# Down projection of a decoder layer's feed-forward part: where VectorE takes the bank sums, who makes the weight sums, and when the weight blocks are requested

## What is computed

```python
    mix = jnp.concatenate([y_a, y_b, y_c], axis=-1) @ p['w_out'][l]
    x = x + rmsnorm(mix, p['g_post_mix'][l])
    h = rmsnorm(x, p['g_pre_ffn'][l])
    f = (jax.nn.silu(h @ p['w_gate'][l]) * (h @ p['w_up'][l])) @ p['w_down'][l]
    x = x + rmsnorm(f, p['g_post_ffn'][l])
```

## Time and profile before

| | |
|---|---|
| profiled execution, device time | 1510.76 us |
| its span in the profile | 1509.1 us |
| down projection, steps 0 to 65 | 1227.7 to about 1451 us |
| fourth product in passes, and the end | 1451.8 to 1509.1 us |
| PE busy, whole span | 94% |
| DVE, ACT, POOL busy, whole span | 61%, 35%, 38% |
| mean granted TensorE clock | 0.969 |

### The profile page before, as it was taken

The page is one execution under the profiler, slowest core; times in us unless marked ns, Lnnn a source line. Parts: engine busy times, 40 slices in busy tenths (PEclk is TensorE's granted clock), DMA queues, the critical chain, the costliest instruction groups (busy, mean ns, idle before and its releaser), DMA issues.

```text
span 1509.1 us, 32359 instructions
## 1 busy us (share of the span) xinstructions
PE 1412.9 (94%) x13256; PEld 1317.4 (87%) x13256; DVE 926.6 (61%) x1441; ACT 521.3 (35%) x914; POOL 579.1 (38%) x493
## 2 busy tenths in 40 slices
PE   7999999997999999889969999999999998888995
PEld 6899999996999665548869999999999998887995
DVE  6439888722888446556686455555555564569866
ACT  5422231222332435444452323333332333333452
POOL 4044000004985222200065555555555530249634
PEclk9999999998999999989989999999999999999997
DMA  7222111222543434452202333333333335554533
GB/s 221 64 46 57 31 43 44 65 61 64 155 115 114 137 85 136 124 170 84 88 24 78 98 93 106 106 96 88 106 106 106 106 114 175 154 154 147 157 85 127
DMA packets 145115, 155.76 MB, mean 103 GB/s; under 512 B 18893, under 2 KB 113352, under 8 KB 144953
## 3 DMA queue, kind: packets, MB, share of 16 engines
q1 hardware_dynamic: 117762, 140.44, 30.7%
q10 hardware_dynamic: 24006, 12.12, 3.0%
q0 software_dynamic: 3200, 1.14, 0.6%
HBM read 120.62 MB, written 33.35 MB: 102 GB/s over the span
## 4 chain that ended last, share of the span: by engine, by line
PE 45%; DVE 5%; POOL 2%; issue 2%; ACT 1%; DMA 1%; SPq 0%; DVEq 0%; POOLq 0%; ACTq 0%
PE mf_ps L3167 28%; PE mf_ps L3194 9%; PE mf_ps L3102 6%; PE mf_ps L3207 1%; POOL ff_a L2635 1%; DMA ff_m_raw<-hidden_operands 1%; PE mf_ps L3225 1%; DVE ff_s_lo L2943 0%; DVE h_lo L2891 0%; POOL ff_a L2639 0%; DVE ff_m_lo L2941 0%; DVE ff_p_lo L2937 0%; DVE ff_scaled L2982 0%; PE mf_ps L3112 0%; DVE h_t_lo L2891 0%
## 5 line engine op out<-in xcount | busy, mean ns | idle before, releaser
L3167 PE MATMUL mf_ps<-h_t_hi,ff_w_hi 128*128 128x258 f32 x704 | 144.5, 287 | 8.8 <-DVE h_t_lo L2891 6.3
L3167 PE MATMUL mf_ps<-h_t_hi,ff_w_lo 128*128 128x258 f32 x704 | 142.9, 285 | 0.0
L3167 PE MATMUL mf_ps<-h_lo,ff_w_hi 128*128 128x258 f32 x704 | 142.4, 284 | 0.0
L2886 DVE TENSOR_TENSOR ff_w_lo<-ff_sum,ff_w_hi 128x512 fp32r<-128x512 f32 x88 | 87.2, 991 | 85.9 <-ACT ff_w_hi L2720 83.9
L3194 PE MATMUL mf_ps<-ff_m_hi,ff_s_hi 128*128 128x258 f32 x528 | 111.0, 293 | 22.0 <-DVE ff_acc L2951 10.7
L3167 PEld LDWEIGHTS mf_ps<-h_t_hi,ff_w_hi 128*128 128x128 f32 x704 | 110.9, 192 | 9.4 <-issue 6.5
L813 PE MATMUL pc_main<-h_hi,in_whi 128*128 128x344 f32 x528 | 116.7, 330 | 1.7 <-PEq L88 1.7
L2941 DVE TENSOR_TENSOR ff_m_lo<-ff_m_raw,ff_m_hi 128x516 fp32r<-128x516 f32 x66 | 75.2, 1140 | 65.3 <-ACT ff_m_hi L2753 64.8
L813 PE MATMUL pc_main<-h_lo,in_whi 128*128 128x344 f32 x528 | 113.2, 323 | 0.0
L813 PE MATMUL pc_main<-h_hi,in_wlo 128*128 128x344 f32 x528 | 112.7, 322 | 0.0
L3167 PEld LDWEIGHTS mf_ps<-h_t_hi,ff_w_lo 128*128 128x128 f32 x704 | 110.4, 191 | 0.0
(11 more groups left out here) (494 smaller groups left out, 3626.0 us busy)
## 6 DMA issues: line engine op xcount, KB each, us to landing
ff_m_raw<-hidden_operands SPq DMA_DIRECT2D x66, 258.0 KB, 3.1
fs_keys<-in_cache_k_dram SPq DMA_DIRECT2D x64, 192.0 KB, 2.9
at_values<-in_cache_v_dram SPq DMA_DIRECT2D x64, 192.0 KB, 2.5
hidden_operands<-ff_t_sum SPq DMA_DIRECT2D x44, 258.0 KB, 3.4
ff_raw<-in_w_gate_dram SPq DMA_DIRECT2D x22, 512.0 KB, 5.9
ff_raw<-in_w_up_dram SPq DMA_DIRECT2D x22, 512.0 KB, 5.2
ff_a<-in_w_down_dram SPq DMA_DIRECT2D x44, 256.0 KB, 3.0
in_raw<-in_w_in_dram ACTq DMA_DIRECT2D x20, 512.0 KB, 3.9
```

The costliest lines, as they stand in the source:

```text
L2886: dve.tensor_tensor(w_lo[q % 4][:], stationary(*tasks[q]), w_hi[q % 4][:].bitcast(F32), ALU.subtract).then_inc(w_lo_cut, 1)
L3167: last = pe.matmul(into[:, g], a[q % 4][:, k], b[:, k, g * TQ:(g + 1) * TQ], start=(fresh and k == 0 and i == 0), stop=(k == KH - 1 and i ...
```

## The change

Six things are changed, all in the down projection:

1. At the end of the products FIRST, SECOND, SEVENTH, SIXTH and THIRD, VectorE's `product_out` stands one low-part step earlier: ahead of the low parts of step j + 2, where it stood behind those of step j + 3 (j the product's last step). ScalarE's `fifth_out` moves in the same way. The addition in SBUF that follows the fifth product stays.
2. The 44 stationary sums go from GpSimd to VectorE, one in each iteration (`sum_blocks(j + 4)`), at its head.
3. Weight blocks have semaphores of their own (`block_in`) and are requested three steps ahead, behind the moving operand of the step and not ahead of it.
4. ScalarE casts the stationary block before the moving operand, and VectorE makes their low parts in that order. ScalarE waits itself for the end of step j - 4.
5. The transposes of chunks (`turned_after`) come one or two pass steps earlier.
6. The statistics (`stats_after`) come one to three pass steps earlier.

```diff
         cut_through = lambda j: min(STEPS, j + 4 + max(0, min(3, j - WIDE + 1)))
-        arrived = lambda j: 32 * (j // 4 + 1) if j < 4 * pairs else 32 * pairs + 16 * (j // 4 + 1 - pairs)
+        LEAD = 3
...
-        turned_after = {68: 0, 69: 1, 73: 2, 74: 3, 80: 4, 81: 5, 85: 6}
-        stats_after = {69: 0, 76: 1, 81: 2, 85: 3}
+        turned_after = {67: 0, 68: 1, 72: 2, 73: 3, 78: 4, 79: 5, 83: 6}
+        stats_after = {68: 0, 73: 1, 80: 2, 84: 3}
...
         def wait_stationary(eng, j):
             k = j % pairs
-            if j // pairs == SEVENTH:
+            if j // pairs in (FIRST, SECOND):
+                eng.wait_ge(block_in[j % 8], 16 * (j // 8 + 1))
+            elif j // pairs == SEVENTH:
                 eng.wait_ge(s3_done, k + 1)
...
+                def load_block(j):
+                    f, half = ((0, 0), (1, 0), (0, 1), (1, 1))[j // pairs]
+                    n = feature(j % pairs, f)
+                    sp.dma_start(blocks[j // pairs][j % pairs][:], m.w_down[
+                        0, n * P:(n + 1) * P, half * KH * P:(half + 1) * KH * P]).then_inc(block_in[j % 8], 16)
...
-                    if j < 4 * pairs:
-                        f, half = ((0, 0), (1, 0), (0, 1), (1, 1))[j // pairs]
-                        n = feature(k, f)
-                        sp.dma_start(blocks[j // pairs][k][:], m.w_down[
-                            0, n * P:(n + 1) * P, half * KH * P:(half + 1) * KH * P]).then_inc(step_in[s], 16)
                     sp.dma_start(m_raw[s][:], m.ops_dram[OPERAND[j // pairs], k]).then_inc(step_in[s], 16)
...
-                load_step(0)
-                load_step(1)
+                for j in range(2):
+                    load_block(j)
+                    load_step(j)
                 sp.wait_ge(multiplied, place[NF - 1, 2] + 1)
+                for j in range(2, 2 + LEAD):
+                    load_block(j)
                 for j in range(2, STEPS):
                     load_step(j)
+                    if j + LEAD < 4 * pairs:
+                        load_block(j + LEAD)
...
-                for k in range(pairs):
-                    third_stationary(k)
-                for k in range(pairs):
-                    second_stationary(k)
-                    if k >= 5:
-                        first_stationary(k - 5)
-                for k in range(pairs - 5, pairs):
-                    first_stationary(k)
                 for n in range(KH):
                     pool.wait_ge(added, 4 * SIXTH + n + 1)
                     pool.tensor_tensor(c21(n), c21(n), c12(n), ALU.add).then_inc(u3_summed, 1)
-                for k in range(pairs):
-                    pool.tensor_tensor(a12[k][:], a12[k][:], a21[k][:], ALU.subtract).then_inc(s4_done, 1)
...
-                    act.wait_ge(step_in[s], arrived(j))
-                    act.copy(m_hi[s][:], m_raw[s][:]).then_inc(step_hi, 1)
+                    if j >= 4:
+                        act.wait_ge(down_done, 4 * (j - 3))
                     wait_stationary(act, j)
                     act.copy(s_hi[s][:], own_block(j)).then_inc(step_hi, 1)
+                    act.wait_ge(step_in[s], 16 * (j // 4 + 1))
+                    act.copy(m_hi[s][:], m_raw[s][:]).then_inc(step_hi, 1)
...
                 for j in range(STEPS):
+                    if j == THIRD * pairs - 2:
+                        for n in range(KH):
+                            fifth_out(j + 1, n)
                     for ahead in range(cut_through(j - 1), cut_through(j)):
                         cut_step(ahead)
...
-                    if j == THIRD * pairs - 1:
-                        for n in range(KH):
-                            fifth_out(j, n)
...
+                    dve.tensor_tensor(s_lo[s][:], own_block(j), s_hi[s][:].bitcast(F32), ALU.subtract).then_inc(step_lo, 1)
+                    dve.wait_ge(step_hi, parts(j))
                     dve.tensor_tensor(m_lo[s][:], m_raw[s][:], m_hi[s][:].bitcast(F32), ALU.subtract).then_inc(step_lo, 1)
-                    dve.wait_ge(step_hi, parts(j))
-                    dve.tensor_tensor(s_lo[s][:], own_block(j), s_hi[s][:].bitcast(F32), ALU.subtract).then_inc(step_lo, 1)
+
+                def sum_blocks(j):
+                    k = j % pairs
+                    if j // pairs == SEVENTH:
+                        dve.wait_ge(block_in[j % 8], 16 * (j // 8 + 1))
+                        dve.tensor_tensor(a21[k][:], a11[k][:], a21[k][:], ALU.subtract).then_inc(s3_done, 1)
+                    elif j // pairs == SIXTH:
+                        dve.wait_ge(block_in[j % 8], 16 * (j // 8 + 1))
+                        dve.wait_ge(step_lo, parts(SEVENTH * pairs + k))
+                        dve.tensor_tensor(a21[k][:], a22[k][:], a21[k][:], ALU.subtract).then_inc(s2_done, 1)
+                    elif j // pairs == FIFTH:
+                        dve.wait_ge(s2_done, k + 1)
+                        dve.tensor_tensor(a11[k][:], a21[k][:], a11[k][:], ALU.add).then_inc(s1_sum_done, 1)
+                    elif j // pairs == THIRD:
+                        dve.tensor_tensor(a12[k][:], a12[k][:], a21[k][:], ALU.subtract).then_inc(s4_done, 1)
...
                 for j in range(STEPS):
+                    if j + 4 < WIDE:
+                        sum_blocks(j + 4)
+                    if j < WIDE and j % pairs == pairs - 2 and j // pairs != FIFTH:
+                        for n in range(KH):
+                            product_out(j + 1, n)
                     for ahead in range(cut_through(j - 1), cut_through(j)):
                         cut_step(ahead)
-                    if j % pairs == pairs - 1:
+                    if j % pairs == pairs - 1 and (j >= WIDE or j // pairs == FIFTH):
                         for n in range(KH):
                             product_out(j, n)
```

13 lines of the change are left out of this document (1 added, 12 removed).

## The result

The changed kernel takes 1483.7 us (median of 4 runs, 1479.4 to 1485.2), the kernel before 1507.9 us in the same rounds; the ratio is 0.984, 95% interval 0.981 to 0.986. The forecast was 1487. The profiled execution took 1485.2 us, its span is 1483.6.

The account below looks back on a forecast made before the run. TensorE, busy 94%, was taken as the bound, with time to win only in its waits and lower clock. Wide products gain 20.9 us, passes lose 1.5: 19.4 us off the 1506.8 median gives 1487, range 1475 to 1499.

Parts of the forecast that it names:

- main line: Whole kernel: the forecast of 1487 us, with late waits at step 58 and before step 77; chance 0.55.
- rival A: Late waits don't come: 1479 us without that at step 58, 1473 without that at step 77 as well; chance 0.22.
- the forecast's own sign of being wrong: Third product: no wait of TensorE at step 58 would show the forecast wrong.
- Bank sums ahead: Changes of product: bank sums no longer wait behind low parts, so TensorE's waits of 3.1, 4.1, 4.3 and 0.8 us go.
- plain loss: Each of six wide products: 0.4 us beyond 31.9 us and its waits, kept in the forecast.
- Step 10: Wait of 1.6 us for the operand behind the last stores: requested earlier, 0.4 us of it kept.
- Start of the fifth product: VectorE's low parts of step 45 slow beside GpSimd's quarter additions: a wait taken as 1.2 us, where 6.6 was.
- Start of the third product: VectorE slowed beside GpSimd's quarter sums: 5.5 us wait at step 58, 1.9 us of lower clock, 0.4 us after.
- The lead at nothing: Wide products: requesting weight blocks three steps ahead costs 0, bounds -1 and +2 us.
- The moved sums: 44 weight sums on VectorE: 0.7 us of small waits go in the sixth product, 6.6 us at the fifth's start shrinks.
- The passes: From step 66: 4.0 us and 1.9 us of clock lost before step 77, 2.5 and 1.9 won later; 1.5 us worse.
- The lower clock at 1.9 us a wait: After long waits TensorE restarts at 1.2 GHz, costing 1.1 to 2.5 us, mean 1.9.

Follow-up runs that it names:

- e7: Kernel before with only the bank sums and ScalarE's fifth-product copies moved ahead of the low parts at a change of product: 1489.2 us, ratio 0.988.
- e3: Changed kernel with the bank sums and ScalarE's copies put back behind the low parts at every change of product: 1493.6 us, ratio 0.990.
- e4: Changed kernel with weight blocks requested in their own step, not three steps ahead: 1492.7 us, ratio 0.990.
- e5: Changed kernel with VectorE also waiting, behind the additions at the third product's start, until GpSimd's first quarter sum is done: 1488.3 us, ratio 0.987.
- e2: Changed kernel with the 44 sums of weight blocks put back on GpSimd: 1494.0 us, ratio 0.991.

## Why the prediction was right

The sign, the places of the gain and the mechanism at four of the five changes of product were right; the gain was 24.2 us for a forecast 19.4. What came is not the main line but the first half of rival A (1479): the forecast's own sign of being wrong, no wait at step 58, is there. That the time lies so near 1487 is in part luck. The wide part gained 30.0 us for a forecast 20.9, and a third of that difference is hidden in the profiled execution by a late start of step 0 and a longer tail.

- **Bank sums ahead** (waits of 3.1, 4.1, 4.3, 0.8 go): right, shown by e7 and e3. The products of the earlier trace rows were to be 32.3 us; they are 31.9. The 0.4 us a product that I carried over as plain loss weren't there: 2.4 us of the difference. A part of them belonged to the waits: where waits of 2.0 and 2.8 us came back in e3 without the lower clock, the products are 0.2 us longer than 31.9 and their waits.
- **Step 10** (0.4 of 1.6 us kept): nothing is left in this profile, and it is the lead that does it (1.5 in e7, 1.2 in e4, 0 to 0.6 in the profiles with the lead).
- **Start of the fifth product** (1.2 us): the window is 0.9 us over 31.9, a wait of 0.6.
- **Start of the third product** (5.5 us at step 58, 1.9 of clock, 0.4 behind): this is the term that was mis-sized. It was 7.8 us, and the window is 1.8 us over 31.9, with waits of 0.9 and 0.3 and no lower clock. The rate of 1.7 us beside GpSimd was right (1.75 to 1.79 us after). Wrong was the start: I took from the earlier trace rows that the additions themselves run at the shared pace and that GpSimd gets in with the first. It was held off for 11.3 us, and the sum for step 59 and the two low parts of step 58 were done at full pace before it got in. Where it was let in, the wait is there: 4.4 us in e5, 3.1 in e2, 1.0 in e3. It was rival A, by a cause I hadn't named. Where the engines did alternate, an instruction of VectorE's took 1.76 us (e5), as in the rows. By the Trainium skill's rule (SBUF — State Buffer, Who interferes with whom) it was to be 1.9 us and the wait 6.1; the runs show neither.
- **The lead at nothing**: wrong as a price of the part by itself in this kernel (9.7 us, e4), right in the sum, which had the blocks landed before the sums ask for them.
- **The moved sums** (0.7 us and a part of the 6.6): too low. With the order alone two products are still 3.0 and 4.7 us too long (e7), and putting the sums back costs 10.3 us of wide part (e2).
- **The passes**: forecast 1.5 us worse, 2.2 in this profile. The second pass was to start 24.2 us after step 66 and starts at 23.9; its wait is 3.4 for 4.6; last wait 0.7 and last transposes 1.97 us for 0.6 and 1.8. The three low parts before the bank sums took 1.07 us and not 3.4, a second hold: GpSimd's residual sums began at 1445.48, and the first of them lasted 4.3 us, until VectorE had done these and the bank sums. So the near hit on the start of the pass is luck: the scaling ahead of the three low parts ended 22.4 us after step 66 for a forecast 20.3, and these 2.1 us too late cancel the 2.3 us that the low parts were too early.
- **The lower clock at 1.9 us a wait**: a mean of something that comes or stays away. The same 3.4 us wait cost 2.3 us in one execution and nothing in another.

The terms add up: (7.8 - 1.8) + 2.4 + 0.4 + (1.2 - 0.9) = 9.1 us, and the wide part took 194.1 us for the 203.2 forecast. The tail's 0.7 us more and the 2.3 us of scatter ahead of step 0 take 3.0 back: the span gained 6.1 us more than forecast.
